# A mixed attention, convolution and expert step: the input projection in another order, with all the convolution in it

## The chip, the cores and the metric

One Trainium2 chip, of which this program uses one core. The metric is the device time of one execution in microseconds (us). The engines are TensorE (PE in the profile, its weight loads PEld), VectorE (DVE), ScalarE (ACT), GpSimd (POOL) and SyncE (SP, which here only starts transfers).

## What is computed

One step of a decoder layer, for a prompt of 1024 tokens (8 tiles of 128) and a sample group of 8 sequences with 4 tokens each, model width 1024, everything in float32. Cut to what matters here:

```
h  = rmsnorm(x) * (1 + scale) + shift          # scale, shift: SiLU(c) @ w_ada, per sequence
q, k, v, ca, cg = split(h @ w_in)              # w_in: 1024 x 2560, five blocks of 512 columns
q, k = rmsnorm per head (8 heads x 64)
glu  = ca * sigmoid(cg)                        # the gated blocks
att  = stick-breaking attention (sigmoids and running products, no softmax), causal
cv   = silu(layernorm(causal depthwise conv(glu, width 31, 512 channels)))
x    = x + gate * (concat(att, cv) @ w_out)
x    = x + gate2 * MoE(...)                    # 16 experts, top 2, within one of four groups
```

The sample group uses the same weights, attends to 1024 cached positions for each sequence, and its convolution starts from a stored state. Keys, values and the last 30 glu rows are outputs too.

## The kernel before

Each engine runs one instruction list, written out by hand, and the lists meet only in semaphore waits; there is no planner. An engine that waits holds up all that stands behind the wait in its list. That holds for SyncE's list of transfers too. The stages, in the profiled run: projection 0 to 358 us, attention 358 to 592, merge with w_out and router 592 to 760, experts 760 to 1233.

**Start.** SyncE loads c, bias rows, x tile 0, then the first half of the adaLN weights for shift and scale (four transfers of 1 MB, `load_early(0, ...)`, line 455), then w_in in eight slabs of 128 rows (1280 KB each, line 467), between them the second half of the adaLN weights (these wait for `ada_used`, since they overwrite the first half's buffers) and x tile 1, then small constants. TensorE computes the first-half rows (`ada_early`, lines 1305 and 1336: `x @ w` with only 32 stationary columns), turns tile 0 of the normed x (`turn_h`, 1355) and the rows (`turn_rows`); VectorE prepares the rows (`early_rows`, 1932 to 1936); ScalarE writes `hT`, the modulated and transposed tile (`evac_hT`, 975). Tile 0 runs with the slab index k outermost (1441), so that five banks accumulate while w_in arrives.

**Tiles 1 to 7** (line 1461) go block by block in the order `CHUNKS = (3, 4, 0, 1, 2)`, that is ca, cg, q, k, v: eight products of 128x128 stationary `hT` by 512 columns of w_in for each block, which the trace shows as 16 records. After ca and cg the list has `turn_post(t-1)`: the glu tile of the tile before is turned in four 128x128 transposes (1368), and its normed q and k in eight (1376). After q it has `turn_h(t+1)`. Behind each block stands one slice of the late adaLN products (`ada_late`, 1316; 32 in all).

For each tile ScalarE takes sigmoid(cg) (1039), stores glu, q and k turned (1000, 1007), squares q and k (1050) and copies v (1056). VectorE multiplies the glu (1977), reduces the squares (1984), scales q and k (2002) after GpSimd's power (800), and GpSimd multiplies the norm weights in (808). The result `qk_done` is what `turn_post` waits for.

**The convolution** is on VectorE, one instruction per tap, 128-channel block and 256 columns of tokens (`conv_taps`, 1957: `out = src * weight + out`). `conv_part(t, part)` spreads the first three quarters of the tokens over tiles 2 to 7, between the reduce and the scale and behind them. The last quarter is `conv_tap` (2113), in attention's loop of 16 cycles: one or two taps of four instructions a cycle, and five taps of channel blocks 2 and 3 that were left over; the last five taps stand behind attention, between the layer norm steps of the first half (`ln_eps`, `ln_diag`, `ln_scale`, `ln_swish`, 2162 to 2182).

**The end of the projection** is `sample_chunks` (1402, 128 small products), `turn_post(7)` and `turn_post(8)`. Before attention's first scores TensorE waits for `qk_var`, `late_rows` and `qk_scaled` of the sample tile, all of them from VectorE. VectorE then lays out the sample queries (2045) and comes to the first running product (`scan`, 2062).

**An attention cycle** has scores (1495) on TensorE, two sigmoids (1090, 1103) on ScalarE, running product and weighting (2062, 2072) on VectorE, transposes (1523), their copy (1113), and values (1535), besides pages of the sample cache (1545, 1123, 1558, 1578).

## Time and profile before

| | us |
|---|---|
| median of 3 timed runs | 1232.38 (1232.27 to 1235.27) |
| the profiled execution, first to last instruction | 1233.3 |
| TensorE busy | 1154.7 (94%) |
| VectorE busy | 600.7 (49%) |
| ScalarE busy | 336.7 (27%) |
| GpSimd busy | 254.3 (21%) |

The profile is of one execution; its span is all that is known of that execution's time, so span and timed median are 0.9 us apart. A busy share counts the time in which an engine has an instruction in work. Matmul records overlap, so their mean length (598 ns for 128x512) is longer than the distance from one to the next. What counts for this change is not the whole-run share but the share in each stage, and what each engine waits for there.

### The profile page before, as it was taken

Reading aid. Unit: us, or ns where it says so; the run is one execution under the profiler, and the core shown is the slowest. Engines: PE = TensorE matmul, PEld = TensorE weight load, DVE = VectorE, ACT = ScalarE, POOL = GpSimd, SP = SyncE. Lnnn points to the kernel's source line nnn. Section 1 sums busy time; section 2 is a strip of 40 time slices with the busy share of each in tenths; the row PEclk is TensorE's granted clock in tenths of the full one; section 3 lists DMA queues with packets and bytes.
Section 4 is the critical chain, followed back from the end, with each engine's and each line's share of the span. In section 5 each row is a group of like instructions: output and inputs, shape, how many; then the busy total and the mean of one; then the engine's idle time right before and its main releaser. Section 6 shows DMA issues by size and latency. Waiting matters only on the chain.

```text
span 1233.3 us, 19314 instructions
## 1 busy us (share of the span) xinstructions
PE 1154.7 (94%) x6769; PEld 540.8 (44%) x6769; DVE 600.7 (49%) x1161; ACT 336.7 (27%) x713; POOL 254.3 (21%) x312
## 2 busy tenths in 40 slices
PE   6999999999989899998999966999999999999996
PEld 4444444444446666665444433333333333333332
DVE  0010867786779999997965357111211211212212
ACT  2132221222138888887212221000000000000000
POOL 2011101221049600000100001123222222232322
PEclk9999999999999999999999986999999999999998
DMA  9843333322347465645833246996789878976663
GB/s 359 332 144 103 103 103 107 97 88 86 90 155 259 142 210 170 205 138 210 311 117 110 91 150 237 375 380 244 262 283 326 312 243 281 367 233 240 219 221 119
DMA packets 115859, 253.37 MB, mean 205 GB/s; under 512 B 15054, under 2 KB 29518, under 8 KB 114760
## 3 DMA queue, kind: packets, MB, share of 16 engines
q1 hardware_dynamic: 94241, 208.42, 48.6%
q0 software_dynamic: 17568, 39.35, 9.1%
q10 hardware_dynamic: 3984, 4.72, 1.1%
q8 instruction: 41, 0.67, 0.2%
q14 instruction: 25, 0.20, 0.0%
HBM read 399.77 MB, written 39.22 MB: 356 GB/s over the span
## 4 chain that ended last, share of the span: by engine, by line
PE 83%; DMA 5%; ACT 4%; issue 4%; DVE 3%; SPq 0%; ACTq 0%; POOL 0%; POOLq 0%; DVEq 0%
PE bank L1784 20%; PE bank L1461 20%; PE bank L1798 10%; PE bank L1652 8%; PE bank L1441 3%; PE bank L1495 2%; PE bank L1535 2%; PE bank L1545 2%; PE bank L1523 2%; PE bank L1774 2%; PE bank L1316 1%; DMA big<-in_w_up_dram 1%; DMA big<-in_w_down_dram 1%; PE bank L1558 1%; ACT mid L1123 1%
## 5 line engine op out<-in xcount | busy, mean ns | idle before, releaser
L1784 PE MATMUL bank<-big,mid 128*64 128x512 f32 x1232 | 283.1, 600 | 2.2 <-DMA big<-in_w_up_dram 1.7
L1461 PE MATMUL bank<-big 128*128 128x512 f32 x560 | 249.2, 598 | 0.1
L1461 PEld LDWEIGHTS bank<-big 128*128 128x128 f32 x560 | 103.7, 190 | 131.2 <-issue 131.2
L1784 PEld LDWEIGHTS bank<-big,mid 128*64 128x64 f32 x1232 | 87.1, 138 | 161.4 <-issue 160.5
L1957 DVE SCALAR_TENSOR_TENSOR cvT<-low,cw,cvT 128x256 f32<-128x256 f32 x360 | 156.9, 510 | 0.0
L1798 PE MATMUL bank<-big,mid 128*64 128x512 f32 x608 | 133.8, 592 | 1.2 <-DMA big<-in_w_down_dram 1.2
L2062 DVE TENSOR_TENSOR_SCAN big<-big 128x513 f32<-128x513 f32 (+4 forms) x96 | 90.2, 978 | 8.2 <-ACT big L1090 8.1
L2485 DVE TENSOR_TENSOR xt<-xt,bank 128x512 f32<-128x512 f32 x20 | 13.8, 688 | 148.5 <-ACT xt L1258 148.5
L2504 DVE TENSOR_TENSOR mid<-bank,low 128x512 f32<-128x512 f32 x38 | 24.5, 686 | 120.0 <-PE bank L1798 79.9
L1798 PEld LDWEIGHTS bank<-big,mid 128*64 128x64 f32 x608 | 44.0, 137 | 87.8 <-issue 87.8
L800 POOL TENSOR_TENSOR st<-st,mhalf 128x16 f32<-128x16 f32 (+1 forms) x9 | 25.2, 2801 | 252.6 <-DVE st L1988 243.9
L1253 ACT ACTIVATE mid<-bank 128x512 f32<-128x512 f32 x20 | 11.9, 597 | 209.2 <-PE bank L1774 209.2
L1652 PE MATMUL bank<-mid,cvT 128*128 128x512 f32 x128 | 56.6, 596 | 1.1 <-DVE cvT L2165 1.1
L899 POOL DMA_INDIRECT out_dram<-mid,o_col x19 | 19.1, 1004 | 184.8 <-DVE mid L2506 184.8
L1652 PE MATMUL bank<-mid,big 128*128 128x512 f32 x128 | 56.9, 596 | 0.0
L1090 ACT ACTIVATE big<-bank,nbb 128x512 f32<-128x512 f32 (+3 forms) x96 | 50.8, 585 | 17.0 <-PE bank L1501 12.1
L1523 PE MATMUL bank<-identf,big 128*128 128x128 f32 x288 | 45.8, 286 | 8.5 <-ACT big L1113 3.3
L2072 DVE TENSOR_TENSOR big<-big 128x512 f32<-128x512 f32 (+3 forms) x96 | 53.3, 592 | 0.4
L1103 ACT ACTIVATE big<-bank,bb 128x512 f32<-128x512 f32 (+3 forms) x96 | 51.2, 600 | 0.0
L2113 DVE SCALAR_TENSOR_TENSOR cvT<-low,cw,cvT 128x256 f32<-128x256 f32 x120 | 50.7, 487 | 0.0
L1270 ACT ACTIVATE mid<-bank 128x512 f32<-128x512 f32 x19 | 11.3, 597 | 139.7 <-PE bank L1791 139.7
L975 ACT ACTIVATE big<-bank,low 128x128 f32<-128x128 f32 x64 | 23.3, 465 | 91.4 <-PE bank L1355 56.8
(341 smaller groups left out, 1349.7 us busy)
## 6 DMA issues: line engine op xcount, KB each, us to landing
big<-in_w_gate_dram SPq DMA_DIRECT2D x42, 2048.0 KB
big<-in_w_up_dram SPq DMA_DIRECT2D x41, 2048.0 KB
big<-in_w_down_dram SPq DMA_DIRECT2D x41, 2048.0 KB
low<-in_w_ada_dram SPq DMA_DIRECT2D x32, 512.0 KB, 4.2
low<-in_cache_v_dram SPq DMA_DIRECT2D x64, 256.0 KB
big<-in_w_in_dram SPq DMA_DIRECT2D x8, 1280.0 KB, 17.1
xt<-in_x_prompt_dram SPq DMA_DIRECT2D x16, 512.0 KB, 4.7
mid<-in_w_ada_dram SPq DMA_DIRECT2D x8, 1024.0 KB, 13.9
```

The costliest lines, as they stand in the source:

```text
L1090: nc.scalar.activation(keep[w][h][:, first:first + n], bank[:, 2 * (i % 2) + h, 0:n], ACT.Sigmoid, scale=-(HD ** -0.5), bias=nbb[:, 2 * pa ...
L1103: nc.scalar.activation(sig[w][h][:, b0 * P:b1 * P], bank[:, 2 * (i % 2) + h, 0:n], ACT.Sigmoid, scale=HD ** -0.5, bias=bb[:, 2 * pair + h: ...
L1441: mm = pe.matmul(bank[:, cc, :], hT[:, 0, k, :], w_in_sb[:, k, cc * 512:(cc + 1) * 512], start=(k == 0), stop=(k == KD - 1))
L1461: mm = pe.matmul(bank[:, 4 if cc == 2 else cc, :], hT[:, s, k, :], w_in_sb[:, k, cc * 512:(cc + 1) * 512], start=(k == 0), stop=(k == KD - 1))
L1523: mm = pe.transpose(bank[:, TURN_BANK["a", 2 * i + h], (kb - b0) * P:(kb - b0 + 1) * P], sig[u % 2][h][:, kb * P:(kb + 1) * P], identf[:, :])
L1652: mm = pe.matmul(bank[:, 2 * (t % 2) + cc, :], cat[:, k % NPAIR, t * P:(t + 1) * P], w_out_sb[:, k, cc * 512:(cc + 1) * 512], start=(k == ...
L1784: mm = pe.matmul(bank[half, 2 * s + w, :], xgT[:, s, k, half], moving, start=(k == 0), stop=(k == KD - 1))
L1798: mm = pe.matmul(bank[half, 6 + w, :], actT[:, s, k, half], wd_sb[:, x, k, w * 512:(w + 1) * 512], start=(k == 0), stop=(k == KF - 1))
L1957: c.put(V.scalar_tensor_tensor(out, src, cw[:, ch, tap:tap + 1], out, ALU.mult, ALU.add))
L2062: V.tensor_tensor_scan(kept, kept, kept, 1.0, ALU.mult, ALU.bypass).then_inc(S["scan_done"], 1)
L2072: V.tensor_tensor(sig[w][h][:, b0 * P:b1 * P], sig[w][h][:, b0 * P:b1 * P], keep[w][h][:, first + b0 * P:first + b1 * P], ALU.mult).then_i ...
L2113: c.put(V.scalar_tensor_tensor(out, x, cw[:, ch, tap:tap + 1], out, ALU.mult, ALU.add))
```

## The change

- **Loads.** x tiles 0 and 1 are loaded ahead of the first-half adaLN weights and tiles 2 and 3 between their two pairs (four x rows are held now). w_in comes in two parts: its columns of ca and cg in eight slabs of 512 KB early (`load_w_conv`), those of q, k and v in four transfers behind the constants (`load_w_qkv`).
- **Start on TensorE.** The list begins with `turn_h(t, 0)` for t = 0 to 3, and only then `ada_early(0, 0)`, `ada_early(0, 1)`, `turn_rows(0)`. ScalarE squares and norms all four tiles; ScalarE writes `hT` of tiles 0 and 2, VectorE that of 1 and 3 (`evac_hT`).
- **Gated blocks.** ca and cg are computed transposed: 128 columns of w_in stationary, 512 tokens (four tiles) moving (`glu_piece`, 8 products of 128x512). Eight pieces for tiles 0 to 3 come before any q, k or v; eight for tiles 4 to 7 come between `qkv(4)` and `qkv(5)`. glu comes out with channels on partitions, so the 32 glu transposes and their copies (1000) are gone; one group of four transposes makes the last 30 rows for the output (`turn_conv_row`).
- **q, k, v** take three pieces a tile (`qkv(t)`), q and k in banks that alternate between tiles. The late adaLN slices are laid out over the 32 pieces behind the first eight.
- **Convolution.** A tap is one instruction per channel block and 512 columns, 248 in all instead of 496. All of it stands in the projection, by the table `CONV`: 22 to 30 in each of tiles 0 to 4, 24 beside the second gated blocks, 28 in each of tiles 5 to 7, 8 ahead of the sample tile's glu, and 8 behind its `late_rows`, ahead of its scaling. Attention's loop and what follows it have no taps.

The core of it, VectorE's part and TensorE's order:

```diff
-                        out = cvT[:, ch, n0:n0 + 2 * P]
-                        src = glu_x[:, ch, n0 + tap:n0 + tap + 2 * P]
+                        out = cvT[:, ch, n0:n0 + GW]
+                        src = glu_x[:, ch, n0 + tap:n0 + tap + GW]
...
+            CONV = {(0, 0): [(0, EVEN, 0, 6)], (0, 1): [(0, EVEN, 6, 11)],
+                    (1, 0): [(0, EVEN, 11, 18)], (1, 1): [(0, EVEN, 18, 23)],
+                    (2, 0): [(0, EVEN, 23, 30)], (2, 1): [(0, EVEN, 30, CW), (0, ODD, 0, 4)],
+                    (3, 0): [(0, ODD, 4, 11)], (3, 1): [(0, ODD, 11, 16)],
+                    (4, 0): [(0, ODD, 16, 23)], (4, 1): [(0, ODD, 23, CW)],
+                    (5, 0): [(1, EVEN, 12, 20)], (5, 1): [(1, EVEN, 20, 26)],
+                    (6, 0): [(1, EVEN, 26, CW), (1, ODD, 0, 3)], (6, 1): [(1, ODD, 3, 9)],
+                    (7, 0): [(1, ODD, 9, 17)], (7, 1): [(1, ODD, 17, 23)]}
+            GLU_CONV = {2: (0, 6), 3: (6, 12)}
...
+            for t in range(GT):
+                var_x(t)
+            for hf in range(2):
+                early_rows(hf)
+                evac_hT(1, hf)
+                evac_hT(3, hf)
...
             for t in range(NTP):
...
+                if t == GT + 1:
+                    late_rows(3)
+                    for ch in range(NCH):
+                        if ch in GLU_CONV:
+                            conv_taps(1, EVEN, *GLU_CONV[ch])
+                        glu(1, ch)
                 conv_part(t, 0)
...
+                conv_part(t, 1)
+            conv_taps(1, ODD, 23, 27)
...
             late_rows(NADA - 1)
+            conv_taps(1, ODD, 27, CW)
...
-                for tap in range(TAPS_BY[cy], TAPS_BY[cy + 1]):
-                    conv_tap(tap)
...
+            def glu_piece(g, c, w, k0=0, k1=KD):
+
+                out_bank, col = GLU_BANK[g][c][w], 3 * AW + w * CC + c * P
+                for k in range(k0, k1):
+                    if g == 0:
+                        pe.wait_ge(w_in_in[k], 16)
+                    mm = pe.matmul(bank[:, out_bank, :], w_in_sb[:, k, col:col + P], hT[:, k, :],
+                                   start=(k == 0), stop=(k == KD - 1))
+                if k1 == KD:
+                    mm.then_inc(S["mm_chunk"], 1)
...
+            for t in range(GT):
+                turn_h(t, 0)
+            ada_early(0, 0)
             ada_early(0, 1)
             turn_rows(0)
...
+            pe.wait_ge(S["hT_sb"], 2)
+            pe.wait_ge(S["hT_dve"], 2)
+            for w in range(2):
+                glu_piece(0, 0, w, 0, KD // 2)
+            turn_h(0, 1)
+            turn_h(1, 1)
+            for w in range(2):
+                glu_piece(0, 1, w, 0, KD // 2)
+            ada_early(1, 0)
+            ada_early(1, 1)
...
+            for t in range(GT + 1):
+                qkv(t)
...
+                for w in range(2):
+                    glu_piece(1, c, w)
...
+            for t in range(GT + 1, NTP):
+                qkv(t)
             sample_chunks()
             turn_post(NTP - 1)
-            turn_post(NTP)
+            turn_sample_glu()
```

## Rows read from the trace of the kernel before

**Rows 1.** Stages: start:end, length; busy PE, PEld, DVE, ACT, POOL; clock, DMA share, GB/s.
```profile
67.50:358.00 290.50, 290.44 (x1102) 130.78 (x1102) 183.31 (x408) 60.48 (x126) 47.80 (x23) 1.00 0.32 97
...
382.66:437.84 55.18, 50.20 (x583) 34.35 (x584) 52.32 (x84) 46.38 (x107) 37.69 (x41) 1.00 0.58 198
437.84:493.01 55.17, 50.19 (x582) 34.31 (x584) 51.27 (x103) 46.37 (x107) 0.00 (x0) 1.00 0.55 184
```

**Rows 2.** The same view, two stretches of 4 us at the start.
```profile
4.00:8.00 4.00, 1.99 (x24) 1.50 (x24) 1.21 (x1) 0.30 (x2) 3.56 (x18) 1.00 1.00 387
8.00:12.00 4.00, 2.69 (x44) 1.69 (x48) 0.15 (x1) 2.66 (x5) 0.58 (x1) 1.00 1.05 392
```

**Rows 3.** Timeline of the start: start, length, engine, line, operation, count, idle before.
```profile
10.46 1.15 ACT L964 ACTIVATE big<-xt,st 128x1024 f32<-128x1024 f32 x1 [0.95 <-POOL st L792]
...
11.89 1.94 PE L1336 MATMUL bank<-mid,cT 128*32 128x128 f32 x32 [0.76 <-DMA mid<-in_w_ada_dram]
...
15.66 0.65 PE L1305 MATMUL bank<-low,ones_row 1*32 1x128 f32 x8
...
16.24 3.64 PE L1336 MATMUL bank<-mid,cT 128*32 128x128 f32 x64
...
21.49 1.50 ACT L975 ACTIVATE big<-bank,low 128x128 f32<-128x128 f32 x4 [9.88 <-DVE low L1936]
...
23.09 17.39 PE L1441 MATMUL bank<-big 128*128 128x512 f32 x36 [2.16 <-ACT big L975]
```

**Rows 4.** TensorE groups by shape, 67.5 to 360: busy, mean ns, idle before.
```profile
L1368 PE MATMUL bank<-identf,mid 128*128 128x128 f32 x33 | 5.2, 275 | 0.0
```

**Rows 5.** VectorE groups by shape, whole run, same columns.
```profile
L2243 DVE SCALAR_TENSOR_TENSOR low<-low,st 128x1024 f32<-128x1024 f32 x8 | 10.3, 1284 | 4.7 <-POOL st L852 4.7
```

**Rows 6.** Timeline of a steady tile of the projection.
```profile
206.70 11.96 DVE L1957 SCALAR_TENSOR_TENSOR cvT<-low,cw,cvT 128x256 f32<-128x256 f32 x30
...
220.49 1.02 ACT L1050 ACTIVATE mid<-bank 128x1024 f32<-128x1024 f32 x1 [2.93 <-PE bank L1461]
...
223.06 3.14 POOL L800 TENSOR_TENSOR st<-st,mhalf 128x16 f32<-128x16 f32 x1 [32.58 <-DVE st L1988]
...
226.23 1.23 DVE L2002 TENSOR_TENSOR mid<-bank,st 128x1024 f32<-128x1024 f32 x1
...
227.38 10.89 DVE L1957 SCALAR_TENSOR_TENSOR cvT<-low,cw,cvT 128x256 f32<-128x256 f32 x22
227.54 2.53 POOL L808 TENSOR_TENSOR mid<-mid,qkw 128x1024 f32<-128x1024 f32 x1 [0.82 <-DVE mid L2002]
...
228.02 0.64 PE L1316 MATMUL bank<-low,cT 128*32 128x256 f32 x8
...
228.59 7.13 PE L1461 MATMUL bank<-big 128*128 128x512 f32 x16
...
235.65 0.64 PE L1316 MATMUL bank<-low,cT 128*32 128x256 f32 x8
```

**Rows 7.** Timeline of the end of the projection.
```profile
348.76 8.80 PE L1402 MATMUL bank<-big 128*32 128x384 f32 x128
...
357.94 0.29 DVE L2014 TENSOR_TENSOR mid<-bank,mid 128x128 f32<-128x128 f32 x1 [0.40 <-ACT mid L1065]
...
365.71 2.60 DVE L2062 TENSOR_TENSOR_SCAN big<-big 128x512 f32<-128x512 f32 x2 [0.26 <-ACT big L1090]
```

**Rows 8.** The chain of waits in attention: start, length, what.
```profile
382.66 1.90 PE bank L1535 x32
...
404.34 1.93 PE bank L1558 x32
...
493.01 1.90 PE bank L1535 x32
...
514.69 1.93 PE bank L1558 x32
```

**Rows 9.** Timeline behind attention.
```profile
610.30 14.00 PE L1652 MATMUL bank<-mid,cvT 128*128 128x512 f32 x32 [1.11 <-DVE cvT L2165]
```

More of the change, by code:

```diff
@@ L194, in decoder_step @@
         G0 = NCH * GX
+        x_row = [xt[:, t, :] for t in range(2)] + [glu_x[:, NCH - 2 + t, TAIL:TAIL + D] for t in range(2)]
+        x_row += [xt[:, t % 2, :] for t in range(GT, NT)]
         glu_s = low[:, G0:G0 + NCH * DB * SX].rearrange("p (c b n) -> p c b n", c=NCH, b=DB)
@@ L343, in decoder_step @@
         x_in = [sem(f"x_in{i}") for i in range(2)]
+        x_mid = [sem(f"x_mid{i}") for i in range(2)]
+        qkv_in = [sem(f"qkv_in{i}") for i in range(KD // 2)]
         kv_st = [sem(f"kv_st{i}") for i in range(2)]
@@ L506, in _ @@
             assert n_const[0] == 16 * N_CONST
+            for i in range(KD // 2):
+                load_w_qkv(i)
+            for t in (GT, GT + 1):
+                sp.wait_ge(S["hT_ps"], t + 1)
+                load_x(t)
             sp.wait_ge(S["modT_ps"], 2)
@@ L1380, in turn_sample_qk, with turn_sample_glu @@
+            def turn_sample_glu():
+                pe.wait_ge(S["glu_done"], NCH * NGRP + 1)
+                pe.wait_ge(S["v_done"], NTP)
+                pe.transpose(bank[:, V_BANK, 0:P], smp_glu, identf[:, :]).then_inc(S["post_ps"], 1)
             def turn_sample_qk():
@@ new lines, in qkv_piece @@
+            def qkv_piece(t, j):
+                n0 = t % GT * P
+                for k in range(KD):
+                    if t == 0:
+                        pe.wait_ge(qkv_in[k // 2], 16)
+                    mm = pe.matmul(bank[:, V_BANK if j == 2 else QK_BANK[t % 2] + j, :], hT[:, k, n0:n0 + P],
+                                   w_in_sb[:, k, j * 512:(j + 1) * 512], start=(k == 0), stop=(k == KD - 1))
+                mm.then_inc(S["mm_chunk"], 1)
+                for n in late_chunks(piece(t, j)):
+                    ada_late(n)
@@ new lines, in _ @@
+            pe.wait_ge(S["hT_sb"], GT)
+            pe.wait_ge(S["hT_dve"], GT)
+            for w in range(2):
+                glu_piece(0, 0, w, KD // 2)
+            turn_taps()
+            for w in range(2):
+                glu_piece(0, 1, w, KD // 2)
+            turn_state(0)
+            glu_piece(0, 2, 0, KD // 2)
+            glu_piece(0, 2, 1)
+            turn_state(1)
+            pe.wait_ge(S["glu_done"], 1)
+            glu_piece(0, 3, 0)
+            pe.wait_ge(S["st_sb"], 1 + 2 * NCH)
@@ new lines, in _, with qkv @@
+            glu_piece(0, 3, 1)
+            def qkv(t):
+                if t >= GT:
+                    pe.wait_ge(S["hT_sb"], GT + 2 * (t - GT + 1))
+                if t < 2:
+                    pe.wait_ge(S["glu_done"] if t else S["sg_done"], NCH if t else 1)
+                elif t < GT + 1:
+                    pe.wait_ge(S["qk_scaled"], t - 1)
+                    pe.wait_ge(S["qk_sq"], t - 1)
+                else:
+                    pe.wait_ge(S["glu_done"], min(2 * NCH, NCH + t - 2))
+                    pe.wait_ge(S["qk_scaled"], t - 1)
+                    pe.wait_ge(S["qk_sq"], t - 1)
+                qkv_piece(t, 0)
+                if t >= 1:
+                    turn_post(t - 1)
+                qkv_piece(t, 1)
+                if GT <= t + 3 < NT:
+                    for hf in range(2):
+                        turn_h(t + 3, hf)
+                if t == NTP - 2:
+                    turn_conv_row()
+                if t == 0:
+                    pe.wait_ge(S["glu_done"], 2)
+                else:
+                    pe.wait_ge(S["v_done"], t)
+                qkv_piece(t, 2)
@@ L1969, in _ @@
+            GLU_CONV = {2: (0, 6), 3: (6, 12)}
+            def conv_part(t, part):
+                for run in CONV[t, part]:
+                    conv_taps(*run)
+            for t in range(GT):
+                var_x(t)
+            for hf in range(2):
+                early_rows(hf)
+                evac_hT(1, hf)
+                evac_hT(3, hf)
             dve.wait_ge(S["pool_const"], 2)
+            for ch in range(NCH):
+                glu(0, ch)
             for t in range(NTP):
                 s = t % 2
-                dve.wait_ge(S["sg_done"], t + 1)
@@ L2102, in evac_o_s @@
                         .then_inc(S["s_o"], 1)
-            def conv_tap(tap):
-                n0 = SEQ - 2 * P
-                for ch in range(NCH):
-                    out, x = cvT[:, ch, n0:SEQ], glu_x[:, ch, n0 + tap:SEQ + tap]
-                    if tap == 0:
-                        c.put(V.tensor_scalar(out, x, cw[:, ch, 0:1], cw[:, ch, CW:CW + 1], ALU.mult, ALU.add))
-                    else:
-                        c.wait(back=NCH - 1)
-                        c.put(V.scalar_tensor_tensor(out, x, cw[:, ch, tap:tap + 1], out, ALU.mult, ALU.add))
             def ln_center(j, in_bank):
@@ L2192, in _ @@
                 c.put(V.scalar_tensor_tensor(m2[:, 1, :], m2[:, 1, :], 1.0, g, ALU.add, ALU.mult))
-            conv_tap(CW - 3)
             ln_swish(0)
-            for tap in range(CW - 2, CW):
-                conv_tap(tap)
             c.wait()
-            dve.sem_inc(S["conv_done"], 1)
             c.reset()
```

489 lines of the change are left out of this document (241 added, 248 removed).

## The prediction

> **What bounds the kernel now.** I read the windows by stage first, then the timeline of the start and of one tile, then the end of the projection, and last the chain of waits in attention, since the change takes work out of one stage and puts it into another.
>
> In the projection TensorE is busy for 290.44 of 290.50 us and VectorE for 183 [rows 1]: TensorE sets the pace, and a tap costs nothing as long as VectorE keeps up. The reader should see in [rows 6] that a block of products (7.06 us from its start to the next group, 228.59 to 235.65) and a late adaLN slice (0.57 us, 228.02 to 228.59) follow each other without a gap. In attention VectorE is the busiest engine by the windows, 51 to 52 us of 55.2, with TensorE at 50 and ScalarE at 46 [rows 1]. That seems to promise much for taking its taps away. The chain says otherwise. Two points one and a half cycles apart (382.66 and 404.34) are 21.68 us apart, and eight cycles later the same two points (493.01 and 514.69) are again 21.68 us apart [rows 8]. By the code the first pair has one tap a cycle (four instructions), the second two taps and two left-over instructions (ten). Six more instructions a cycle moved nothing by a hundredth, and the chain's pieces there are TensorE's and ScalarE's. At the start TensorE has small adaLN products until 19.88 and its first projection product at 23.09, released by ScalarE's copy of the turned tile [rows 3].
>
> **The change, part by part.** I add up how much later the first running product of attention starts (365.71 before, [rows 7]), then what comes off behind it. Base is the profiled execution, 1233.3 us; the timed median is 0.9 less.
>
> *Start.* Before, the second adaLN transfer released TensorE at 11.89, when x tile 0 and two transfers of 1 MB were in (2.62 MB) [rows 3]. x tile 3 now has 4.19 MB up to its end. The other 1.57 MB at 0.39 MB/us [rows 2] take 4.0 us: 15.9. ScalarE then squares it and norms tiles 2 and 3, three passes of 1.15 us [rows 3]: 19.4. TensorE's list has these transposes (some 1 us) ahead of the adaLN products, so the two halves of those, which took 15.66 to 19.88 = 4.2 us each with their bias [rows 3], end at 20.4 + 8.4 = 28.8 instead of 19.88. Rows, transposes and copy took 3.2 us (19.88 to 23.09), and ScalarE now copies two tiles, 1.5 us more [rows 3]: first projection product at 33.5, **10.4 us later**. From both sides: 5, if the small products run in a shorter time once the engine is in work without a break, and 12, if the transfers are slower. The 4 MB for the second adaLN half still arrive ahead of their use, because the slabs of w_in ahead of them are 2 MB instead of 5, and q, k, v columns are wanted only at about 100 us. I cost both at nothing.
>
> *TensorE's work.* Products: 8 x 5 x 8 before, 2 x 4 x 2 x 8 + 8 x 3 x 8 = 320 after, the same. Of 32 glu transposes 28 go; 33 of them were busy for 5.2 us [rows 4], so at most 4.4 and, without each group's tail, some 3.5: **4.0 us less**. ScalarE's and VectorE's waits for transposed tiles in the first group and the split pieces come out about even with the gap that tile 0 had; 0 to 2 either way. `sample_chunks` so starts at 348.76 + 10.4 - 4.0 = 355.2, and TensorE is through with it (8.8 us, [rows 7]) and with `turn_post(7)` at 365.0.
>
> *VectorE in tiles 5 to 7.* The trace has no tap of 512 columns. 30 taps of 256 take 11.96 us, 0.40 each [rows 6]; the same operation on 1024 columns takes 1.284 [rows 5]. Half-way by columns, and without the tail that a single instruction shows, gives 0.66 for 512; 0.60 and 0.70 are its ends. Behind the scaling GpSimd multiplies for 2.53 us, and 22 taps there take 10.89 instead of 8.77 [rows 6]: they are held for 2.1 us a tile. From the end of ScalarE's square (221.51) to the end of the scaling (227.46) are 5.95 us, most of it GpSimd's power [rows 6]; 5.7 where VectorE comes late to the reduce. A tile of 24 taps costs VectorE 15.8 + 2.1 + 5.7 = 23.6 us, of 28 taps 26.3. TensorE needs 3 x 7.06 + 3 x 0.57 + 16 transposes of 0.12 = 24.8. So it is level through tile 4 and VectorE falls behind from 5.
>
> Counted out: from the start of tile 5 to `sample_chunks` TensorE has 9 blocks (63.5), 8 late slices (4.6) and 36 transposes (4.3), 72.4, so tile 5 starts at 282.8. Its square ends 16.2 later (two blocks, turned q and k, 1.02), its scaling at 305.0. Then VectorE has 76 taps (12 + 16 + 12 + 16 + 12 + 8: 50.2 us), three holds (6.3) and the rounds of tiles 6 and 7 (11.4) until the sample's glu: 372.9. TensorE is there at 365.0 and stands in `turn_sample_glu`: **8 us of new wait**. Queued behind it are the first scores, which also wait for VectorE's `late_rows` and sample scaling. From the sample's glu to the first running product took 7.77 us (357.94 to 365.71) [rows 7]; the 8 taps in front of the scaling add 8 x 0.66 = **5.3 us**, of which GpSimd's power hides nothing that is not already inside the 7.77. The first running product is at 372.9 + 7.8 + 5.3 = 386.0, **20.3 us later**. With 0.60 a tap it is 5 less, with 0.70 3 more.
>
> *Attention.* Taps gone: 0, by the equal distances of [rows 8]. Windows show one dip of the clock in cycle 11 there which need not come again; I take 0.8 off.
>
> *Behind attention.* TensorE's second half of the merge is released by VectorE's swish at 610.30 [rows 9]. Two groups of four taps (1.6 us each by [rows 6]) stood on that way, one of them beside ScalarE's sigmoids: 1.4 less; 0 and 3.2 are the ends. From there on TensorE is the bound, and experts are not touched.
>
> Sum: 1233.3 + 20.3 - 0.8 - 1.4 = 1251.4 in the profile, 0.9 less for the median: **1250.5**.
>
> **Rivals.**
> 1. *VectorE keeps pace*: the 512-column tap is nearer to 0.55, or GpSimd's hold is met by fewer, longer instructions. Then the 8 us of wait go and the rest stays: 1242.5. For it: the tiles are within 2 us of level. Against: one element a cycle shows in both widths.
> 2. *Attention was VectorE's after all.* Mechanism: the running products of a cycle start when VectorE is free of taps, so the cycle shrinks to the next engine, ScalarE's 46.4 of 55.2 [rows 1]. Over 16 cycles that is 4 x 8.8 = 35 us: 1250.5 + 0.8 - 35 = 1216. It ends on the faster side from about 1.2 us a cycle on (18.9 / 16). For it: VectorE is at 95% there. Against: [rows 8]. The Trainium skill, page "Perfetto Trace Analysis", section "Identifying the Most-Contended Engine", says for VectorE to take occupancy as the sign of the bottleneck and to optimise that engine first; by that rule this rival is the likeliest outcome. Here the chain of waits speaks against the rule.
> 3. *The start is covered*: x tile 3 and its norms don't hold the adaLN products, only the longer copy and the transposes remain (2.5 us instead of 10.4): 1242.5. Against: `turn_h(3, 0)` stands first in TensorE's list.
>
> **How the numbers follow.** Forecast 0.60, its own range 1243 to 1258 (tap length, start). Rival 1 0.16, rival 3 0.10, rival 2 0.14, of which most is the full or half effect (faster), a little ends within 0.3% (3.7 us, about what a measurement of this kernel can tell from no change). Rivals 1 and 3 together would give 1234.5, still in or beside that band. So faster 0.13, same 0.07, slower 0.80. The range runs from 1233 to 1259: below it lies most of rival 2, above it a start and a tap length both at their bad ends.
>
> **What would show it.** First projection product near 33 us instead of 23. Taps of 0.66 us from one to the next, and a stretch of 2 us without progress behind each scaling. TensorE idle for some 8 us at the sample glu's transpose and some 5 to 6 more at the first scores, its releaser VectorE. First running product near 386. Distances in attention of 21.68 us as before, with VectorE's busy share down to about 80%. The prediction is wrong if attention's cycles get shorter by over 1 us, or if VectorE is at the sample's glu ahead of TensorE.

## The result, and the profile of the changed kernel

| | before | changed |
|---|---|---|
| timed runs of this comparison, us | 1232.49 (1232.27 to 1235.27, 4 runs) | 1254.16 (1252.32 to 1257.46, 4 runs) |
| the profiled execution, first to last instruction | 1233.3 | 1250.6 |
| granted clock in that execution, mean over the span | 0.976 | 0.971 |

The ratio is 1.0171, with a 95% interval of 1.015 to 1.0193: the change makes this kernel slower. Forecast were 1250.5 us, 1233 to 1259, and 0.80 for slower. The two profiled executions are 17.3 us apart, the medians 21.7; the steps are compared between the profiles. Wherever both are on record for one execution, the timed value is at least 1.7 us above the span. So before's span of 1233.3 fits only the slowest of its timed runs (1235.27), while the changed kernel's profiled execution is the fastest of its own (1252.32).

The windows of the changed kernel (columns as in [rows 1]): the projection, and twice four cycles of attention.

```profile
98.30:353.00 254.70, 254.70 (x892) 111.02 (x894) 184.94 (x261) 45.99 (x83) 45.39 (x20) 1.00 0.32 98
400.03:455.20 55.17, 50.20 (x582) 34.31 (x584) 45.77 (x68) 46.38 (x107) 38.88 (x41) 1.00 0.50 171
455.20:510.40 55.20, 50.24 (x583) 34.35 (x584) 37.71 (x67) 46.28 (x107) 0.00 (x0) 1.00 0.56 183
```

TensorE is busy without a break from 98 to 353 us, as it was before. In attention VectorE fell from 51 to 52 us of 55.2 to 46 and 38, and the stretch is as long as in [rows 1]. The chain of waits there (start, length, what), at the points that answer to [rows 8]:

```profile
400.03 1.90 PE bank L1651 x32
...
421.71 1.93 PE bank L1674 x32
...
510.36 1.90 PE bank L1651 x32
...
532.04 1.93 PE bank L1674 x32
```

21.68 us from the first to the second and from the third to the fourth: the same to a hundredth as before. So nothing of attention got shorter. The loss must lie elsewhere, most of it before 400 us, where this stretch begins 17.4 us late. The timeline of the start (as in [rows 3]):

```profile
17.26 2.17 ACT L1011 ACTIVATE low<-low,st 128x1024 f32<-128x1024 f32 x2
...
18.45 2.15 PE L1413 MATMUL bank<-identf,low 128*128 128x128 f32 x8 [4.25 <-ACT low L1011]
...
21.11 3.30 PE L1395 MATMUL bank<-mid,cT 128*32 128x128 f32 x64
...
24.69 1.96 PE L1395 MATMUL bank<-mid,cT 128*32 128x128 f32 x64
...
28.25 2.90 ACT L1023 ACTIVATE big<-bank,low 128x128 f32<-128x128 f32 x8 [8.82 <-DVE low L2055]
...
31.20 8.58 PE L1495 MATMUL bank<-big 128*128 128x512 f32 x16 [3.51 <-ACT big L1023]
```

TensorE turns tiles 2 and 3 only when ScalarE has normed them (4.25 us idle before 18.45), the two halves of the adaLN products stand behind, and the first projection product starts at 31.20 instead of 23.09. The end of the projection, which answers to [rows 6] and [rows 7]:

```profile
327.62 20.72 DVE L2091 SCALAR_TENSOR_TENSOR cvT<-low,cw,cvT 128x512 f32<-128x512 f32 x28
...
348.45 1.22 DVE L2131 TENSOR_REDUCE st<-mid 128x16 f32<-128x1024 f32 x1
...
351.56 8.82 PE L1467 MATMUL bank<-big 128*32 128x384 f32 x128
...
352.89 1.22 DVE L2146 TENSOR_TENSOR mid<-bank,st 128x1024 f32<-128x1024 f32 x1 [3.01 <-POOL st L848]
354.03 15.45 DVE L2091 SCALAR_TENSOR_TENSOR cvT<-low,cw,cvT 128x512 f32<-128x512 f32 x20
369.41 0.28 DVE L2156 TENSOR_TENSOR mid<-bank,mid 128x128 f32<-128x128 f32 x1
...
369.74 0.48 PE L1445 MATMUL bank<-identf,mid 128*128 128x128 f32 x1 [8.34 <-DVE mid L2156]
376.64 2.08 PE L1611 MATMUL bank<-big 64*128 64x512 f32 x4 [6.43 <-DVE mid L2174]
...
383.18 2.51 DVE L2205 TENSOR_TENSOR_SCAN big<-big 128x512 f32<-128x512 f32 x2 [0.35 <-DVE xt L2187]
```

Here the reader should follow VectorE. 28 taps take 20.72 us (327.62), and the sum of squares follows them without an idle time of its own (348.45). The scaling comes at 352.89, 20 taps at 354.03 take 15.45, and only then the sample tile's glu can run, at 369.41. TensorE was through with its work at about 361 and stands 8.34 us in front of the glu's transpose (369.74), then 6.43 us in front of the first scores (376.64), which wait for VectorE's scaling of the sample tile behind 8 more taps. The first running product starts at 383.18; before it was 365.71.

Standing cost TensorE a second time, in clock. The seventh column of this window is the granted clock:

```profile
376.60:383.20 6.60, 5.55 (x16) 1.94 (x16) 3.15 (x11) 3.69 (x9) 3.66 (x8) 0.50 0.43 146
```

While TensorE stood, the granted clock fell from 0.97 of full speed (361.4 to 365.5) to 0.50 (365.5 to 369.7), the lower of its two levels, and it stayed there to 383.2. The four products of the first scores took 2.08 us (376.64). In the kernel before the clock was 0.92 from 360.5 to 365.7, and the same four took 1.13 (360.54). From the sample's scaling to the first running product are 7.01 us (376.17 to 383.18) instead of 5.75 (359.96 to 365.71).

Last, the timeline behind attention, which answers to [rows 9]:

```profile
592.88 2.29 DVE L2251 TENSOR_TENSOR cvT<-cvT,bank 128x2048 f32<-128x2048 f32 x1 [7.36 <-PE bank L1710]
...
612.76 1.27 POOL L878 TENSOR_TENSOR big<-cvT 128x512 f32<-128x512 f32 x1
...
612.82 2.89 DVE L2299 TENSOR_SCALAR big<-identf,st 128x128 f32<-128x128 f32 x4 [1.13 <-POOL st L888]
...
614.11 1.32 POOL L880 TENSOR_TENSOR big<-big,cvT 128x512 f32<-128x512 f32 x1
...
615.76 1.12 PE L1801 MATMUL bank<-big,mean_of 128*128 128x512 f32 x2 [0.73 <-DVE big L2299]
...
626.58 14.00 PE L1768 MATMUL bank<-mid,cvT 128*128 128x512 f32 x32 [1.11 <-DVE cvT L2289]
```

The four small operations of `ln_diag` (612.82) take 2.89 us, beside two of GpSimd's sums that start at 612.76 and 614.11. In the kernel before, GpSimd's first sum came long behind them:

```profile
598.06 0.87 DVE L2175 TENSOR_SCALAR big<-identf,st 128x128 f32<-128x128 f32 x4 [1.13 <-POOL st L840]
...
613.55 1.27 POOL L830 TENSOR_TENSOR big<-cvT 128x512 f32<-128x512 f32 x1 [15.53 <-DVEq L2198]
```

There the same four took 0.87.

### The profile page after: what moved, and what is told of

Its sections match the earlier page's. It is cut to its first block, busy times and chain, and to the rows that moved or that the text cites. A ratio compares the mean times of both kernels' runs of the same rounds, so it can differ in the third digit from the quotient of the medians.

```text
span 1250.6 us, 18989 instructions
## 1 busy us (share of the span) xinstructions
PE 1149.9 (92%) x6741; PEld 535.0 (43%) x6741; DVE 579.2 (46%) x929; ACT 328.4 (26%) x690; POOL 257.1 (21%) x312
## 4 chain that ended last, share of the span: by engine, by line
PE 76%; DVE 8%; DMA 5%; ACT 5%; issue 4%; POOL 1%; SPq 0%; ACTq 0%; POOLq 0%; DVEq 0%
PE bank L1900 21%; PE bank L1505 9%; PE bank L1914 9%; PE bank L1495 9%; PE bank L1768 8%; DVE cvT L2091 5%; PE bank L1611 2%; PE bank L1651 2%; DMA big<-in_w_gate_dram 2%; PE bank L1661 2%; PE bank L1639 2%; PE bank L1890 2%; PE bank L1674 1%; DMA big<-in_w_up_dram 1%; ACT mid L1179 1%
## 5 line engine op out<-in xcount | busy, mean ns | idle before, releaser
L2091 DVE SCALAR_TENSOR_TENSOR cvT<-low,cw,cvT 128x512 f32<-128x512 f32 x240 | 177.0, 811 | 0.0
L1505 PE MATMUL bank<-big 128*128 128x512 f32 x384 | 169.8, 595 | 0.0
L1495 PE MATMUL bank<-big 128*128 128x512 f32 x256 | 114.9, 603 | 5.0 <-ACT big L1023 5.0
L1505 PEld LDWEIGHTS bank<-big 128*128 128x128 f32 x384 | 71.1, 190 | 85.0 <-issue 85.0
L1495 PEld LDWEIGHTS bank<-big 128*128 128x128 f32 x256 | 48.0, 192 | 63.5 <-issue 58.0
L1309 ACT ACTIVATE mid<-bank 128x512 f32<-128x512 f32 x20 | 11.9, 597 | 206.8 <-PE bank L1890 196.1
L1611 PE MATMUL bank<-big 64*128 64x512 f32 (+3 forms) x192 | 46.2, 559 | 7.4 <-DVE mid L2174 6.4
```

The costliest lines, as they stand in the source:

```text
L1495: mm = pe.matmul(bank[:, out_bank, :], w_in_sb[:, k, col:col + P], hT[:, k, :], start=(k == 0), stop=(k == KD - 1))
L1505: mm = pe.matmul(bank[:, V_BANK if j == 2 else QK_BANK[t % 2] + j, :], hT[:, k, n0:n0 + P], w_in_sb[:, k, j * 512:(j + 1) * 512], start=(k ...
L1611: mm = pe.matmul(bank[:, 2 * (i % 2) + h, 0:n], stage[64 * h:64 * h + 64, s, 0, qb * P:(qb + 1) * P], stage[64 * h:64 * h + 64, s, 1, b0 * ...
L2091: c.put(V.scalar_tensor_tensor(out, src, cw[:, ch, tap:tap + 1], out, ALU.mult, ALU.add))
```

## The experiments

All edits are to the changed kernel, unless said. "First running product" is VectorE's `scan` that opens attention, "merge" the second half of the merge on TensorE ([rows 9]: 610.30 before; 626.58 changed).

**1. Attention without taps in the kernel before.** The taps in attention and behind it are left out but for tap 0 of the last quarter of the tokens, the left-over ones of channel blocks 2 and 3 among them, so its convolution is incomplete. The loop's lines are shown; the `conv_tap` calls behind attention go too.

```diff
-                if LATE_FROM <= cy < LATE_FROM + CW - LATE_TAP:
-                    tap = LATE_TAP + cy - LATE_FROM
-                    conv_taps(NTP // 2 - 2, (2, 3), tap, tap + 1)
-                for tap in range(TAPS_BY[cy], TAPS_BY[cy + 1]):
+                for tap in range(1 if cy == 0 else 0):
                     conv_tap(tap)
...
-            conv_tap(CW - 5)
...
```

> The kernel before, with the taps in attention and behind it left out (all but tap 0 of the last 256 tokens and the left-over taps of channel blocks 2 and 3), so its convolution is incomplete. It is before's attention with some 128 instructions of 0.4 us, 51 us of VectorE, taken away. My theory (attention is paced by TensorE and ScalarE, distance of the two chain points 21.68 us) expects the cycles unchanged, at most 2 us less behind attention and 1.6 us if the clock dip stays away: 1229 to 1232.5. The rival (attention was VectorE's) expects cycles down towards ScalarE's 46.4 of 55.2 us: 1197 to 1215.

Measured: 1231.78 us (1229.47 to 1239.67), ratio to before 0.9982, interval 0.9963 to 1.0002. One of its windows, its chain, and the merge:

```profile
439.54:494.75 55.21, 50.22 (x582) 34.36 (x584) 37.68 (x67) 46.46 (x107) 0.00 (x0) 1.00 0.59 196
```

```profile
439.54 1.90 PE bank L1535 x32
...
461.23 1.93 PE bank L1558 x32
```

```profile
611.54 14.00 PE L1652 MATMUL bank<-mid,cvT 128*128 128x512 f32 x32 [1.11 <-DVE cvT L2162]
```

VectorE's share falls to 38 of 55.2 us and the distance of the two points is 21.69 against 21.68. Attention is not VectorE's. That closes rival 2, and it means that the change puts its taps into a stage that has to pay for them, out of one that did not. (Behind the merge the router sees other data here, and that stage is 618.2 us instead of 623.0, so the total says even less for the taps than it seems to.) Behind attention the taps were worth half a microsecond: from `ln_center` to the merge are 32.70 us (578.84 to 611.54), 33.19 before (577.11 to 610.30). `ln_diag` comes 1.0 us earlier, but TensorE then has products of the merge in hand, and half of it is lost again.

**2. Taps moved back into attention's cycles.** The last taps of channel blocks 2 and 3, tokens 512 to 1023, go into attention, one tap (two instructions) a cycle for 8 instructions in all, two taps a cycle for 28 and 34. In GpSimd's list the wait for the last tap goes back behind the first sums, where the kernel before has it.

```diff
             late_rows(NADA - 1)
-            conv_taps(1, ODD, 27, CW)
...
+                if cy >= 1 and 27 + (cy - 1) < CW:
+                    conv_taps(1, ODD, 27 + (cy - 1), 27 + cy)
...
```

With 28 the lists `(7, 1)` and the 8 instructions ahead of the glu go too (from tap 17 on), with 34 also three taps of `(7, 0)` (from tap 14 on).

> The changed kernel with the 8 taps behind late_rows (taps 27 to 30 of channel blocks 2 and 3) moved into attention's cycles 1 to 4, two instructions a cycle. Nothing is left out. My theory: first scores wait for the sample's scaling, which stood behind these 5.4 us; GpSimd's power of 1.0 us becomes visible instead of 0.1: 4.8 us earlier, and nothing given back in attention, so 4.8 us less than the changed kernel. The rival (the start of attention is set by something else, such as stores and staged loads) expects no gain.

Measured: 1250.78 us (1248.18 to 1253.02), ratio 1.0135 (1.0117 to 1.0153). From the sample's glu (370.02) to the first running product (378.86) are 8.84 us instead of 13.77, and the span is 1246.4. It is still 1.07 more than the 7.77 of [rows 7]: TensorE had stood 8.34 us for the glu here too, and its first scores again took 2.08 us (372.43).

> As the one above, with 28 instructions moved (taps 17 to 30 of channel blocks 2 and 3), four a cycle in cycles 1 to 7. Nothing is left out. My theory: 4.8 us as above, and TensorE's wait of 8.3 us at the sample's glu goes too, after which TensorE is the bound: 13.1 us less than the changed kernel, about 1240; the 2.7 us of taps a cycle in attention cost nothing. The rival (VectorE paces attention) expects the 18.5 us of taps to come back there: about no gain.

Measured: 1242.36 us (1242.04 to 1250.32), ratio 1.0083 (1.0056 to 1.011), span 1240.3: 10.3 less, not 13.1. The timeline says what is late now:

```profile
348.19 1.22 DVE L2131 TENSOR_REDUCE st<-mid 128x16 f32<-128x1024 f32 x1
...
364.94 1.79 PE L1611 MATMUL bank<-big 64*128 64x512 f32 x4 [3.68 <-DMA big<-out_dram]
...
371.09 2.60 DVE L2202 TENSOR_TENSOR_SCAN big<-big 128x512 f32<-128x512 f32 x2 [0.26 <-ACT big L1146]
...
425.57 5.81 DVE L2091 SCALAR_TENSOR_TENSOR cvT<-low,cw,cvT 128x512 f32<-128x512 f32 x4
...
434.33 1.26 PE L1639 MATMUL bank<-identf,big 128*128 128x128 f32 x8 [0.58 <-DVE big L2212]
```

TensorE's first scores wait 3.68 us for a transfer (364.94), the staged q, k and v. SyncE's list has it behind the stores of tile 7, and those wait for VectorE's sum of squares, which is at 348.19, 3.4 us behind ScalarE's squares. VectorE was late there as well; the longer wait for the sample tile had covered it.

And the taps were not quite free in attention, though that had been expected. Four of them took 5.81 us (425.57) beside GpSimd's layer norm sums, which start at 425.17, where four take 2.73 without such company (439.69). VectorE comes late, and TensorE waits for it twice, 0.58 us at 434.33 and 0.58 at 445.86. Two stretches of four cycles last 55.90 and 55.86 us at a granted clock of 1.00, 1.4 us more than two of 55.17. VectorE is busy for 54.2 of the 55.9 us there, 97%. With 34 moved the same four taps take 5.79, but the wait does not show, since the clock fell at that point (0.97 over 56.77 us) and TensorE was later itself; in the kernels of experiment 7 it is 0.2 us once or twice. So about 1 us of the 2.8 that are missing is the late load, 1 attention (210.7 us from the first running product to `ln_center`, 209.7 in the changed kernel), and 0.8 the stage behind the merge.

> As the run with 28 taps moved back into attention's cycles, but 34: the last six come from tile 7, ahead of its sum of squares. With 28 moved, VectorE came 3.4 us late to that sum (ScalarE's squares end at 344.8, the sum starts at 348.19), the storing of tile 7's q, k and v and behind it the staged load for the first scores followed, and the scores waited for that load until 364.69 (TensorE 3.68 us idle, released by the transfer) while the sample tile was ready at 362.5. Theory: the six taps (4.0 us) are just the 3.4 us by which the sum is late; the load lands near 361.3, the scores start when the sample tile is scaled, and the first running product comes 2.3 to 3.4 us earlier than 371.09; span 1240.3 - 2.8 = 1237.5. Rival (the load waits for something else in SyncE's list, VectorE's taps are no longer on the path): no change, 1240.3. With 2.6 us of taps a cycle attention stays at 55.17 us for each 2.5 cycles of the chain in both.

Measured: 1242.17 us (1240.29 to 1243.69), ratio 1.0071 (1.0054 to 1.0088), span 1238.5.

```profile
345.45 1.22 DVE L2131 TENSOR_REDUCE st<-mid 128x16 f32<-128x1024 f32 x1 [0.70 <-ACT mid L1103]
...
363.62 1.94 PE L1611 MATMUL bank<-big 64*128 64x512 f32 x4 [1.74 <-DVE mid L2172]
...
369.92 2.60 DVE L2202 TENSOR_TENSOR_SCAN big<-big 128x512 f32<-128x512 f32 x2 [0.26 <-ACT big L1146]
```

The sum of squares is 2.7 us earlier, the scores wait for the sample's scaling and no longer for the transfer, and the first running product is 1.2 us earlier. (The expectation calls 55.17 us two and a half cycles; they are four.) The 1.2 us are less than the 2.3 to 3.4 expected: in this execution TensorE's stream up to `sample_chunks` (351.92) ran 0.6 us later than with 28 moved, and TensorE, not VectorE, sets the end of the projection from here on: VectorE has 10.00 us idle ahead of the sample's glu (361.12). The interval of the timed runs overlaps that with 28 moved. From 383.18 to 369.92, 13.3 of the 17.5 us of the late first running product are VectorE's taps in this stage, with what TensorE's standing for them cost in clock.

**3. Narrow taps.** Each tap of 512 columns as two of 256.

```diff
-                        out = cvT[:, ch, n0:n0 + GW]
-                        src = glu_x[:, ch, n0 + tap:n0 + tap + GW]
+                        for m in (n0, n0 + GW // 2):
+                            out = cvT[:, ch, m:m + GW // 2]
+                            src = glu_x[:, ch, m + tap:m + tap + GW // 2]
```

> The changed kernel with each tap of 512 columns as two of 256, 496 instructions instead of 248. The kernel before shows 0.40 us from one 256-column tap to the next, the changed kernel 0.66 to 0.67 for 512. VectorE so has 0.80 - 0.66 = 0.14 us more for each of 248 taps, 34 us in all. Theory (VectorE's tap stream sets the end of the projection since tile 5): in tiles 0 to 4 TensorE's 24.8 us a tile against VectorE's 22 to 30 taps makes VectorE late from tile 0 or 1 on, and as q and k banks alternate it holds TensorE; the first running product (383.18) comes 22 to 34 us later, the span is 1272 to 1285. Rival (the width does not matter because TensorE is the bound until the sample): only the 84 taps from tile 5 on count, 12 us: 1262. If the tap is cheaper at 256 columns than 0.40 when many stand in a row, less.

Measured, one run: 1275.22 us, span 1273.5, 22.9 more. The first running product:

```profile
404.40 2.51 DVE L2206 TENSOR_TENSOR_SCAN big<-big 128x512 f32<-128x512 f32 x2 [0.35 <-DVE xt L2188]
```

It is 21.2 us later, just short of the 22 to 34 and far from the rival's 12. A steady tile with 28 taps lasts 30.0 us in VectorE's list instead of 26.4. Of the 34 us that VectorE has more, about 13 are swallowed where it has idle time, in tiles 0 to 4 and beside the second gated blocks; the excess also shows once on the way, as 8.44 us in which TensorE waits for VectorE ahead of the second group of gated blocks. That VectorE's stream of taps sets the end of this projection is shown from both sides.

**4. The order of the start.**

```diff
-            for t in range(GT):
-                turn_h(t, 0)
+            turn_h(0, 0)
+            turn_h(1, 0)
             ada_early(0, 0)
+            turn_h(2, 0)
+            turn_h(3, 0)
             ada_early(0, 1)
```

> The changed kernel with TensorE's first items in another order: transposes of x tiles 0 and 1, first half of the adaLN rows, transposes of tiles 2 and 3, second half. In the changed kernel the first half runs from 21.11 for 3.30 us, the second from 24.69 for 1.96 us, and the first projection product stands at 31.20. Theory (the transposes of tiles 2 and 3, which wait for ScalarE until 18.45, hold the adaLN products): the first half ends before 18.5, the second starts near 21 and takes 2.0 to 3.3 us, the first product comes 2.4 to 3.7 us earlier, at 27.5 to 28.8, and everything behind it by as much less as VectorE is late at the sample's glu: VectorE's convolution is counted from its own start, which moves too, so the first running product (383.18) comes 1.5 to 3.7 earlier. Rival (the x transfers, not the order, set the start): no earlier than 30.5. Total 1250.6 less 2 to 4 in its profile.

Measured, one run: 1252.0 us, span 1250.2. The timeline, and one window in which the seventh column is the clock:

```profile
14.57 2.62 PE L1395 MATMUL bank<-mid,cT 128*32 128x128 f32 x64
...
19.18 0.65 PE L1413 MATMUL bank<-identf,low 128*128 128x128 f32 x4 [0.38 <-ACT low L1011]
...
22.12 1.08 PE L1395 MATMUL bank<-mid,cT 128*32 128x128 f32 x32 [0.93 <-DMA mid<-in_w_ada_dram]
...
27.76 9.75 PE L1495 MATMUL bank<-big 128*128 128x512 f32 x16 [3.52 <-ACT big L1023]
```

```profile
43.00:60.00 17.00, 15.01 (x173) 8.28 (x172) 3.65 (x11) 3.02 (x8) 0.00 (x0) 0.91 0.77 282
```

The first product came 3.4 us earlier, as expected, but the first running product only 0.5 (382.64), short of the 1.5 to 3.7 expected. At 56.64 us the lead was still 2.3. The granted clock between 43 and 60 was 0.91, where the changed kernel had 1.00, and the 16 products from 56.64 took 8.80 us instead of 7.10: that took 1.7 of it. So this one execution could not tell what the order is worth.

**5. The second adaLN half ahead.**

```diff
+            ada_early(1, 0)
+            ada_early(1, 1)
             turn_h(0, 1)
             turn_h(1, 1)
+            turn_rows(1)
             for w in range(2):
                 glu_piece(0, 1, w, 0, KD // 2)
-            ada_early(1, 0)
-            ada_early(1, 1)
-            glu_piece(0, 2, 0, 0, 2)
-            turn_rows(1)
-            glu_piece(0, 2, 0, 2, KD // 2)
             turn_h(2, 1)
             turn_h(3, 1)
+            glu_piece(0, 2, 0, 0, KD // 2)
```

> The changed kernel with the second adaLN half (product rows for hT's other four slabs) ahead of the transposes and gated pieces it used to follow, so that rows, copies and hT of the second half are made while TensorE has gated pieces. In the changed kernel TensorE stands from 56.34 to 58.91 for ScalarE's copies of hT. Theory: that gap of 2.4 us goes, the q, k, v tiles start 2.4 us earlier and the first running product 1 to 2.4 us earlier. Rival: the weights of the second half are not in by then and the gap moves forward to the adaLN products; nothing is gained. Span 1248.2 by the first, 1250.6 or more by the second.

Measured, one run: 1253.69 us, span 1251.9. TensorE has no idle time between 43 and 60 us (it had 2.0), and the first running product is at 380.77, 2.41 earlier. But in this execution two of attention's stretches had the clock dip that the profile of the changed kernel does not have: from 391.50 to 448.25 are 56.75 us instead of 55.17, and the same again later. Attention so lasts 2.4 us longer, and the stage behind the merge 1.3. The step is worth 2.4 us at the first running product in this execution; the total of one run says nothing on it.

**6. GpSimd's sum behind `ln_diag`.**

```diff
             pool.wait_ge(S["pv_mm"], U)
+            pool.wait_ge(S["ln_diag"], N0["ln_diag"] + LN_DIAGS[0])
             ln_sum(1)
```

> The changed kernel, with GpSimd's ln_sum(1) held back until VectorE's ln_diag(0) is done. Nothing is left out. In the changed kernel ln_diag took 2.89 us for four instructions instead of 0.87, while GpSimd's sums of three 128x512 pairs ran; before, the sums started behind the last taps. If GpSimd's access holds VectorE there, the diag is back at 0.9 us and the kernel 2.0 us faster than the changed one. The rival (the diag is slow for its own reasons) expects no change.

Measured: 1253.37 us (1252.5 to 1254.01), ratio 1.0152 (1.0135 to 1.0169), span 1250.7. The timeline:

```profile
595.00 2.29 DVE L2252 TENSOR_TENSOR cvT<-cvT,bank 128x2048 f32<-128x2048 f32 x1 [7.37 <-PE bank L1711]
...
614.93 0.88 DVE L2300 TENSOR_SCALAR big<-identf,st 128x128 f32<-128x128 f32 x4 [1.13 <-POOL st L888]
...
615.96 1.26 POOL L878 TENSOR_TENSOR big<-cvT 128x512 f32<-128x512 f32 x1 [1.05 <-DVE big L2300]
...
616.99 1.02 PE L1802 MATMUL bank<-big,mean_of 128*128 128x512 f32 x2
...
627.70 14.00 PE L1769 MATMUL bank<-mid,cvT 128*128 128x512 f32 x32 [1.11 <-DVE cvT L2290]
```

`ln_diag` takes 0.88 us again with GpSimd behind it at 615.96. Of the 2.0 us only 1.0 arrives: from `ln_center` to the merge are 32.70 us (595.00 to 627.70), 33.70 without the edit, because TensorE now has products of the merge in hand when `ln_diag` ends and comes to the next item at 616.99. That the spans are equal (1250.7 and 1250.6) is no argument against it: attention had two dips here and took 2.4 us more. The medians, 0.8 us apart, do not tell 1.0 from nothing; the 32.70 us come again in both kernels of experiment 7.

**7. All together.** 34 instructions moved, experiments 4, 5 and 6; and the same without 4.

> All the edits that gained something alone, together: 34 tap instructions moved into attention, the second adaLN half ahead of the pieces, TensorE's first items in the other order, GpSimd's sum behind VectorE's ln_diag. From the single runs: first running product 369.92 with 34 moved, less 2.41 for the second half, less 0.56 for the order (its 3.4 us at the first product were mostly lost again to a lower clock between 43 and 60 us): 367.0 if they add, against 365.71 in the kernel before; tail 1.0 less than in the changed kernel. Theory (the four are the whole loss, and what is left is the later start less TensorE's dropped transposes): span 1238.5 - 3.0 - 1.0 = 1234.5, within 0.5% of the kernel before, ratio 1.000 to 1.006. Rival (the new order of the projection has a cost of its own that no run has shown yet): ratio 1.007 or more, as with 34 moved alone. Faster than before by over 0.3% only if the lower clock behind the start does not come: then 2 to 3 us less.

> As the run with all edits together, but TensorE's first items stay in the changed kernel's order. First running product 369.92 - 2.41 = 367.5, tail 1.0 less, span 1235.1. If the other order is worth its 3.4 us at the first product this one is 2 to 3 us slower than the run with all; if the lower clock behind the start takes it back, as it did when the order was changed alone, they are within 1 us of each other.

Measured, on one chip: all together 1235.22 us (1233.6 to 1236.91, 12 runs), ratio 1.0001 (0.9988 to 1.0013) to before's 1235.12 (23 runs); without the order of the start 1238.93 (1236.49 to 1241.49, 12 runs), ratio 1.0034 (1.0021 to 1.0048). In the profile of all together, and, for the last of the three, the row of the kernel before:

```profile
363.62 2.60 DVE L2204 TENSOR_TENSOR_SCAN big<-big 128x512 f32<-128x512 f32 x2 [0.26 <-ACT big L1147]
...
607.32 14.00 PE L1770 MATMUL bank<-mid,cvT 128*128 128x512 f32 x32 [1.11 <-DVE cvT L2293]
...
778.78 1.09 PE L1902 MATMUL bank<-cvT,mid 128*64 128x512 f32 x1 [4.21 <-DMA big<-in_w_gate_dram]
```

```profile
780.24 0.61 PE L1784 MATMUL bank<-cvT,mid 128*64 128x512 f32 x1 [2.34 <-DMA big<-in_w_gate_dram]
```

The first running product is 2.1 us earlier than before (365.71) and the merge 3.0. The first expert's product has only 1.5 of that: it waits for its gate weights, 4.21 us where before it was 2.34. The rest goes in the experts, and the spans are 1233.4 and 1233.3. The order of the start is worth 3.1 us at the first running product (366.75 without it) and 0.33% in time: what experiment 4 lost to the clock does not come each time. So the first running product is 3.4 us ahead of the 367.0 expected, but the span only 1.1 ahead of the 1234.5, since the stage behind the merge took 626.1 us instead of the 623.0 of before. The four edits give back all of the loss, and no version beats the kernel before.

## Why the prediction was right, step by step

- *What bounds the stages*: right, and shown. Taking VectorE's taps out of attention changed the chain by 0.00 to 0.01 us in either kernel. The Trainium skill's rule ("Perfetto Trace Analysis", section "Identifying the Most-Contended Engine") to optimise the engine with the highest occupancy first is what this case speaks against: in this stage the 95% engine was not on the chain. How near it was, experiment 2 shows: with 28 instructions moved back it was at 97% in one stretch and held TensorE twice. Of the rivals, 2 falls by experiment 1, 1 by the tap's 0.67 us, and 3 by TensorE's 4.25 us of waiting for the normed tiles ahead of 18.45.
- *Start*, +10.4 forecast, +8.1 measured. The mis-sized term is the second adaLN half, taken at 4.2 us with its bias from a row at the slower of two paces; it took 2.3 (24.34 to 26.65). The transfers, squares and norms came as counted (norms until 19.4 forecast, 19.4 measured). Experiment 4 shows the mechanism, the transposes of tiles 2 and 3 ahead of the products. The start is not the same in each execution: in the seven others with this order the first product stands at 29.93 to 31.74.
- *TensorE's work*, 4.0 less forecast. `sample_chunks` starts at 351.56, 2.8 later than before: 8.1 - 2.8 = 5.3 us less, so this term was too small by 1.3, within the 0 to 2 that the prediction left open; what makes it up was not traced. The two errors have opposite signs in the total.
- *The tap*, 0.66 forecast from two other widths: 13 of them take 8.69 us, 0.67 each. The hold beside GpSimd's product, 2.1 forecast: 20 taps in 15.45 us are 2.1 more than 20 x 0.67.
- *VectorE at the sample's glu*, forecast 372.9, measured 369.41; TensorE's wait there 8 and 8.34. VectorE came 3.5 us earlier than forecast and TensorE 3.6 (361.4 instead of 365.0), by the start and TensorE's work, so the difference held. Shown by experiments 2 and 3. What the prediction did not see is that VectorE is late a second time, through tile 7's stores and the staged load; it cost nothing as long as the first wait was longer.
- *Glu to first running product*, 7.8 + 5.3 forecast, 13.8 measured, and 8.8 without the 8 taps. The prediction left out that TensorE stands ahead of it and works on at a granted clock of 0.50: 1.3 us more between scaling and running product. Against that stands the 0.6 us of GpSimd's power that the taps hide. Where TensorE does not stand, in the kernel with all edits, the clock is 1.00 from 358.4 to 363.6, and the 5.75 us of before are 5.67.
- *First running product*, +20.3 forecast, +17.5 measured. The forecast was 2.8 too late there.
- *Attention*, 0, and 0.8 off for a clock dip of the kernel before. Its profile had a stretch of 56.8 us, the changed kernel's had none, so 1.6 came off in this pair. Of the ten kernels of the experiments nine show one or two such stretches in their profile, not always in the same cycle, and that with 28 moved none.
- *Behind attention*, -1.4 forecast, +0.5 measured, from `ln_center` to the merge (33.19 before, 33.70 after). This step of the forecast failed, in two parts. It priced the taps on this way at 1.4 us, and experiment 1 shows 0.5 (33.19 to 32.70). And it took GpSimd's second sum (`ln_sum(1)`) to stay where it was. In GpSimd's list of before a wait for `conv_done`, the last tap, stood ahead of it, so that it ran at 613.55, under the merge; the last tap is now long past, the wait has moved ahead of all sums, and this one starts as soon as attention's last values are there, on `ln_diag`. Experiment 6 shows it: 2.0 us on VectorE, 1.0 on the path. 33.19 - 0.5 + 1.0 are the 33.70 measured, so nothing is left open here. The Trainium skill ("SBUF — State Buffer", section "SBUF: two separate sides") says that GpSimd shares a pair of ports with VectorE, where VectorE's instruction is in a two-port mode or has two inputs in SBUF and GpSimd reads SBUF too; the one that starts first has it for its whole instruction, and the other blocks. The rows agree for the taps, which have two inputs in SBUF (5.81 against 2.73 us for four). For the four scalings of `ln_diag`, 2.89 against 0.87 us fit it; in which mode they ran, no run shows.
- *Behind the merge*: 624.0 us, before 623.0, forecast no difference.

The sum 1251.4 for the profile stands against 1250.6, the median 1250.5 against 1254.16: the medians lie further apart than the profiles, since the profiled execution of the changed kernel is the fastest of its four and that of before fits only its slowest. The step from the profile to the median failed by this: it was put at 0.9 us down, from one pair of numbers of different executions, and was 3.6 up. Some of the closeness is luck: start and first running product too late by 2 to 3 us, dip, tail and end too early by 2.

## What to carry to other kernels

A high busy share promises nothing until the chain of waits runs through that engine: compare two like stretches with different load on it, here one tap against two and a half, before moving work. The place to pay attention to is where the work goes: count the receiving engine's list against the pacing engine, tile by tile, and find the item that stands last in its list, since a backlog of many tiles is paid there at once. Moving it back is not free either: beside GpSimd's sums four taps took twice as long. And when a wait is removed, look for a second one that it had covered, in another engine's queue.

## What the runs showed of the hardware that was not expected

- Two groups of 64 small products of the same shape took 3.30 us (21.11) and 1.96 us (24.69) in one execution, 3.64 and 2.25, 2.59 and 1.96 in others. The windows of the changed kernel show no clock behind it, 1.00 in both:

```profile
21.10:24.30 3.20, 3.20 (x68) 2.82 (x64) 0.00 (x0) 0.00 (x0) 0.00 (x0) 1.00 1.02 408
24.70:26.60 1.90, 1.90 (x68) 1.68 (x64) 0.00 (x0) 0.00 (x0) 0.00 (x0) 1.00 0.95 314
```

  The eight transposes ahead of them were as slow, 2.06 us (12.13) and 2.15 (18.45) against 1.04 (39.63), so the slow pace is TensorE's up to some 24 us in this execution, and not that of these products. What sets it was not tried; a price at the slow pace must not be used twice.
- An earlier start of the projection's products is partly paid in clock. In the five executions with the first product at 30.65 us or later (30.65 to 31.74) the first 16 take 8.58 to 8.83 us, in the five with it at 30.24 or earlier (27.52 to 30.24) 9.75 to 10.17, where a block later takes 7.06 [rows 6]. The granted clock from 27 to 35 us is 0.79 to 0.84 of full speed in the first five and 0.61 to 0.66 in the others. The execution that started 1.2 us earlier than the changed kernel's (29.98) was 0.4 us later behind these 16. Why the clock stays low longer after an earlier start was not looked into.
- Three adds of 128x512 with two inputs on GpSimd (1.3 us each) stretched four scalings of 128x128 on VectorE from 0.87 to 2.89 us. The same was seen with 8, 28 and 34 instructions moved, 2.88 each, and 0.87 to 0.88 in all three kernels in which GpSimd waited. Four taps of 512 columns beside the same kind of adds took 5.8 us instead of 2.7.
- Standing for VectorE for 8.34 and 6.43 us left TensorE at a granted clock of 0.50, and its next scores took 2.08 us instead of 1.13. So a wait of TensorE cost more than its length.
- The stage behind the merge took 622.4 to 626.3 us in kernels that have no edit in it (1246.4 - 623.96 and 1238.2 - 611.95), with other waits for expert weights in each. What sets this was not tried; it is as large as the gain that the last version had at the merge.
